# Half of a branch's activations turned by block moves and VectorE's 32x32 turns, where TensorE transposed them

## What is computed

```
h = rms_norm(x);  z = h @ w_in
u = gelu(z_u);  v = layer_norm(gelu(z_v))
A = u * (W_s v + b)             # per chunk of 128 positions and group of 128 channels
B = multi-head latent attention, 16 heads
x = x + w_out( sigmoid(g_A) * (A @ P_A) + sigmoid(g_B) * (B @ P_B) )
x = x + channel mixer           # dense SwiGLU in layer 0, top 2 of 8 experts in layer 1
```

## Time and profile before

| | |
|---|---|
| median of 3 runs | 1416.42 us |
| the profiled execution | 1416.22 us |
| its span | 1414.5 us |
| TensorE busy | 1406.1 us (99%) |
| VectorE busy | 1166.8 us (82%) |
| ScalarE busy | 951.0 us (67%) |
| GpSimd busy | 170.2 us (12%) |
| DMA | 424.32 MB, mean 300 GB/s |

### The profile page before, as it was taken

How to read it: one execution, slowest core, us unless ns; L and a number is a source line. 1 busy time by engine, 2 the same in 40 slices (tenths; PEclk the granted TensorE clock), 3 DMA queues, 4 the chain that set the end, 5 groups by cost and what they waited for, 6 DMA issues and landing times.

```text
span 1414.5 us, 19105 instructions
## 1 busy us (share of the span) xinstructions
PE 1406.1 (99%) x6575; PEld 1161.6 (82%) x6575; DVE 1166.8 (82%) x1196; ACT 951.0 (67%) x968; POOL 170.2 (12%) x302
## 2 busy tenths in 40 slices
PE   9999999999999999999999999999999999999998
PEld 7888778888888888788888888888888888888886
DVE  6998766676647899667989898898998988989986
ACT  6678645445445677644777787777877777777775
POOL 2032003476500050000300000000000000000010
PEclk9999999999999999999999999999999999999999
DMA  9476548976665484558899999999999999999995
GB/s 335 162 220 207 177 151 329 298 233 201 201 221 187 161 243 130 207 165 327 312 360 410 365 392 409 373 387 407 352 410 384 377 406 372 390 374 394 409 356 204
DMA packets 171587, 424.32 MB, mean 300 GB/s; under 512 B 19388, under 2 KB 50744, under 8 KB 171496
## 3 DMA queue, kind: packets, MB, share of 16 engines
q1 hardware_dynamic: 157128, 393.42, 76.5%
q0 software_dynamic: 13328, 26.16, 6.2%
q10 hardware_dynamic: 1040, 3.68, 0.6%
HBM read 398.20 MB, written 15.81 MB: 293 GB/s over the span
## 4 chain that ended last, share of the span: by engine, by line
PE 95%; DMA 2%; DVE 1%; ACT 1%; issue 1%; POOL 1%; SPq 0%; ACTq 0%; DVEq 0%; POOLq 0%
PE ps L620 87%; DMA raw_more<-in_moe_w_down 1%; PE ps L1187 1%; PE ps L1046 1%; PE ps L1055 1%; PE ps L925 1%; PE ps L1044 1%; PE ps L1030 1%; PE ps L969 1%; ACT w_hi L550 1%; DVE w_lo L555 1%; POOL hid_blocks L881 0%; PE ps L1003 0%; DMA hid_blocks<-hid 0%; PE ps L942 0%
## 5 line engine op out<-in xcount | busy, mean ns | idle before, releaser
L555 DVE TENSOR_TENSOR w_lo<-raw,w_hi 128x2048 fp32r<-128x2048 f32 (+3 forms) x184 | 383.7, 2093 | 81.9 <-ACT w_hi L550 80.6
L550 ACT ACTIVATE w_hi<-raw 128x2048 fp32r<-128x2048 f32 (+3 forms) x184 | 322.3, 1758 | 126.0 <-PE ps L620 102.1
L620 PE MATMUL ps<-w_hi,act_hi 128*128 128x512 f32 (+1 forms) x1264 | 332.4, 391 | 0.1
L620 PE MATMUL ps<-w_hi,act_lo 128*128 128x512 f32 (+1 forms) x1264 | 328.4, 387 | 0.0
L620 PE MATMUL ps<-w_lo,act_hi 128*128 128x512 f32 (+1 forms) x1264 | 326.6, 387 | 0.0
L620 PEld LDWEIGHTS ps<-w_lo,act_hi 128*128 128x128 f32 x1264 | 235.8, 188 | 48.1
L620 PEld LDWEIGHTS ps<-w_hi,act_lo 128*128 128x128 f32 x1264 | 235.6, 188 | 47.9
L620 PEld LDWEIGHTS ps<-w_hi,act_hi 128*128 128x128 f32 x1264 | 233.1, 188 | 46.1 <-ACT act_hi L1330 0.5
L555 DVE TENSOR_TENSOR w_lo<-raw_more,w_hi 128x2048 fp32r<-128x2048 f32 (+1 forms) x96 | 201.8, 2110 | 30.0 <-ACT w_hi L550 30.0
L550 ACT ACTIVATE w_hi<-raw_more 128x2048 fp32r<-128x2048 f32 (+1 forms) x96 | 170.1, 1775 | 54.4 <-PE ps L620 50.7
L555 DVE TENSOR_TENSOR w_lo<-raw_low,w_hi 128x2048 fp32r<-128x2048 f32 (+1 forms) x64 | 137.6, 2156 | 13.7 <-ACT w_hi L550 13.1
(11 more groups left out here) (294 smaller groups left out, 1356.1 us busy)
## 6 DMA issues: line engine op xcount, KB each, us to landing
raw<-in_moe_w_gu SPq DMA_DIRECT2D x96, 512.0 KB, 11.7
raw_more<-in_moe_w_down SPq DMA_DIRECT2D x80, 512.0 KB, 10.2
raw<-in_w_in SPq DMA_DIRECT2D x66, 512.0 KB, 5.3
raw_low<-in_moe_w_gu SPq DMA_DIRECT2D x64, 512.0 KB, 12.0
raw_more<-in_moe_w_gu SPq DMA_DIRECT2D x64, 512.0 KB, 12.5
raw<-in_moe_w_gu SPq DMA_DIRECT2D x48, 384.0 KB, 9.6
raw<-in_dense_w_gu SPq DMA_DIRECT2D x34, 512.0 KB, 5.2
raw_lent<-in_moe_w_gu SPq DMA_DIRECT2D x32, 512.0 KB, 11.4
```

Of the source, the lines that this page charges most:

```text
L550: nc.scalar.activation(w_hi[:, self.split_slot(j), 0:n], self.raw(j)[:, 0:n], ACT.Copy).then_inc(self.hi, 1)
L555: nc.vector.tensor_tensor(w_lo[:, c, 0:n], self.raw(j)[:, 0:n], w_hi[:, c, 0:n].bitcast(F32), ALU.subtract).then_inc(self.lo, 1)
L620: return nc.tensor.matmul(dst, a, b, start=start and n == 0, stop=stop and n == 2)
```

## The change

Half 0 of the branch, in both layers, is no longer transposed by TensorE; half 1 still is. ScalarE writes the biased values of half 0 into `vbuf` in another order of columns (each run of 128 channels cut into four runs of 32, so that the same run of the four groups lies together), and for that waits until both banks of `mix_tokens` are done. VectorE's product of half 0 is made in eight pieces. GpSimd's queue then copies 16 blocks of 32 partitions to `u_buf`, whose first half is free by then, with 32 KB each in runs of 512 bytes. In a new step `a_blocks`, after the argument product of "u" 1 and before the softmax product of pair 1, VectorE transposes the 32 x 32 blocks of these 128 x 1024 elements into a part of `kb`. In a new step `a_split`, at the end of the steps behind the first chunk of "gb" 1, ScalarE copies them to `t1_hi` and VectorE writes the difference to `t1_lo`, in two instructions each. The product "pa" 0 waits for these, not for the turns. Some semaphores of the router are merged into two that count up; their order of events is the same. Left out below are those renamings.

```diff
@@ -213,11 +213,11 @@
         mul(l, "u", 0, 4, [("u_arg", l, 0), split("split_hi"), ("blocks", l, "k", 0), ("u_gelu", l, 0), ("branch", l, 0)],
             split=False)
         mul(l, "u", 1, 0, [*slot(1, exps=False), ("split_lo", l, len(chunks) - 2), split("split_hi")], split=False)
-        mul(l, "u", 1, 4, [("u_square", l, 1), *slot(2, exps=False), ("u_arg", l, 1), ("softmax", l, 1)], split=False,
-            inside=[(2, ("a_turns", l, 0)), (2, ("softmax", l, 0)), (2, ("last_q", l, "q", 1)),
+        mul(l, "u", 1, 4, [("u_square", l, 1), *slot(2, exps=False), ("u_arg", l, 1), ("a_blocks", l, 0), ("softmax", l, 1)], split=False,
+            inside=[(2, ("softmax", l, 0)), (2, ("last_q", l, "q", 1)),
                     (5, ("split_lo", l, len(chunks) - 2)), (5, split())])
         mul(l, "gb", 1, 0, [("values", l, 0), split("split_hi"), *slot(3, values=False, exps=False), ("u_gelu", l, 1),
-                            ("branch", l, 1), ("blocks", l, "k", 1)], split=False, inside=[(4, ("u_tanh", l, 1))])
+                            ("branch", l, 1), ("blocks", l, "k", 1), ("a_split", l, 0)], split=False, inside=[(4, ("u_tanh", l, 1))])
         mul(l, "gb", 1, 4, [("values", l, 1), ("split_lo", l, len(chunks) - 2), *slot(4, values=False, exps=False), split("split_lo"), ("softmax", l, 3), evac("gb", 1)], split=False,
             inside=[(2, ("exps", l, 2)), (5, ("a_turns", l, 1)), (7, ("norm_probs", l, 2)),
                     (7, split("split_hi"))])
@@ -380,6 +380,9 @@
+        branch_moved = u_buf[:].rearrange("p j t n -> p j (t n)").rearrange("p j (t b k i) -> p j t b k i", t=TT, b=4, k=4)
+        branch_turned = kb[:].rearrange("p t g h d -> p (t g h d)")[:, 4 * STRIP:6 * STRIP]
+        branch_by_tile = branch_turned.rearrange("p (t b k i) -> p t b k i", t=TT, b=4, k=4)
@@ -468,6 +471,8 @@
+        a_moved, a_turned, a_hi, a_lo = (
+            [sem(f"a_moved{j}") for j in range(1)], sem("a_turned"), sem("a_hi"), sem("a_lo"))
@@ -625,6 +630,12 @@
+        BY_BLOCKS = 1
+        def branch_by_block(j):
+            return vbuf[:, :, j * STRIP:(j + 1) * STRIP].rearrange("p t (c k i) -> p t c k i", c=4, k=4)
@@ -671,7 +682,7 @@
-                    "pa": lambda: last_turn["a_turns", l, half],
+                    "pa": lambda: None if half < BY_BLOCKS else last_turn["a_turns", l, half],
@@ -858,12 +869,18 @@
+                for j in range(BY_BLOCKS):
+                    pool.wait_ge(branch_a, 2 * l + j + 1)
+                    for b in range(4):
+                        for c in range(4):
+                            pool.dma_start(branch_moved[32 * c:32 * c + 32, j, :, b, :, :],
+                                           branch_by_block(j)[32 * b:32 * b + 32, :, c, :, :]).then_inc(a_moved[j], 16)
-                    nc.gpsimd.memset(zeros, 0.0).then_inc(zeroed, 1)
-                    pool.wait_ge(zeroed, 1)
+                    nc.gpsimd.memset(zeros, 0.0).then_inc(ident_ready, 1)
+                    pool.wait_ge(ident_ready, 4)
@@ -1061,7 +1078,10 @@
+                    blocked = what == "pa" and not j and k0 // 4 < BY_BLOCKS
+                        if blocked:
+                            pe.wait_ge(a_hi, BY_BLOCKS * l + k0 // 4 + 1)
@@ -1089,6 +1109,8 @@
+                        elif p == 1 and not cell and blocked:
+                            pe.wait_ge(a_lo, BY_BLOCKS * l + k0 // 4 + 1)
...
@@ -1439,11 +1461,23 @@
-                            op = nc.scalar.activation(vbuf[:, :, gg * P:(gg + 1) * P],
-                                                      ps[:, 4 + bb % 2, g * S:(g + 1) * S].rearrange(
-                                                          "p (t d) -> p t d", t=TT),
-                                                      ACT.Identity, bias=b_sp[:, l, gg:gg + 1], scale=0.5)
+                            if step[2] < BY_BLOCKS:
+                                if not b and not g:
+                                    act.wait_ge(turn_done, bb + 2)
+                                dst, src = branch_by_block(step[2])[:, :, :, 2 * b + g, :], "p (t c i) -> p t c i"
+                                src = ps[:, 4 + bb % 2, g * S:(g + 1) * S].rearrange(src, t=TT, c=4)
+                            else:
+                                dst = vbuf[:, :, gg * P:(gg + 1) * P]
+                                src = ps[:, 4 + bb % 2, g * S:(g + 1) * S].rearrange("p (t d) -> p t d", t=TT)
+                            op = nc.scalar.activation(dst, src, ACT.Identity, bias=b_sp[:, l, gg:gg + 1], scale=0.5)
+                elif kind == "a_split":
+                    j = step[2]
+                    act.wait_ge(a_turned, BY_BLOCKS * l + j + 1)
+                    for t in range(TT):
+                        op = copy(t1_hi[:, 4 * j:4 * j + 4, t * P:(t + 1) * P].rearrange("p k (b i) -> p k b i", b=4),
+                                  branch_by_tile[:, t].rearrange("p b k i -> p k b i"))
+                    op.then_inc(a_hi, 1)
@@ -1926,9 +1960,30 @@
-                        op = stt(vbuf[:, t, cols], u_buf[:, j, t, :], mix_scale[:, ONE, t:t + 1], vbuf[:, t, cols],
-                                 ALU.mult, ALU.mult)
+                        if j < BY_BLOCKS:
+                            for k in range(4):
+                                v = branch_by_block(j)[:, t, :, k, :]
+                                op = stt(v, u_buf[:, j, t, k * P:(k + 1) * P].rearrange("p (c i) -> p c i", c=4),
+                                         mix_scale[:, ONE, t:t + 1], v, ALU.mult, ALU.mult)
+                        else:
+                            op = stt(vbuf[:, t, cols], u_buf[:, j, t, :], mix_scale[:, ONE, t:t + 1], vbuf[:, t, cols],
+                                     ALU.mult, ALU.mult)
+                elif kind == "a_blocks":
+                    j = step[2]
+                    dve.wait_ge(a_moved[j], 16 * 16 * (l + 1))
+                    if not j:
+                        dve.wait_ge(k_moved[1], 16 * 4 * DG * (l + 1))
+                    nc.vector.transpose(branch_turned, u_buf[:, j].rearrange("p t n -> p (t n)")).then_inc(a_turned, 1)
+                elif kind == "a_split":
+                    j = step[2]
+                    dve.wait_ge(a_hi, BY_BLOCKS * l + j + 1)
+                    for t in range(TT):
+                        k, cols = slice(4 * j, 4 * j + 4), slice(t * P, (t + 1) * P)
+                        op = tt(t1_lo[:, k, cols].rearrange("p k (b i) -> p k b i", b=4),
+                                branch_by_tile[:, t].rearrange("p b k i -> p k b i"),
+                                t1_hi[:, k, cols].bitcast(F32).rearrange("p k (b i) -> p k b i", b=4), ALU.subtract)
+                    op.then_inc(a_lo, 1)
```

More of the change, by code:

```diff
@@ L478, in decoder_trunk @@
         merged_b, sig_done = sem("merged_b"), sem("sig_done")
-        counting_ready, router_ready = sem("counting_ready"), sem("router_ready")
-        zeroed, rows_zeroed, gain_landed, pick_ready, rows_ready, rows_written = (
-            sem("zeroed"), sem("rows_zeroed"), sem("gain_landed"), sem("pick_ready"), sem("rows_ready"),
+        router_ready, routed_by_pe, routed_by_act = sem("router_ready"), sem("routed_by_pe"), sem("routed_by_act")
+        LOGITS_DONE, LOGITS_TURNED, PLACES_DONE = 1, 2, 3
+        COUNTING_READY, LOGITS_COPIED, GAP_EXP = 1, 2, 3
+        rows_zeroed, gain_landed, pick_ready, rows_ready, rows_written = (
+            sem("rows_zeroed"), sem("gain_landed"), sem("pick_ready"), sem("rows_ready"),
             sem("rows_written"))
@@ L486, in decoder_trunk @@
         hid_turned, hid_copied, hid_split = sem("hid_turned"), sem("hid_copied"), sem("hid_split")
-        logits_copied, logits_turned = sem("logits_copied"), sem("logits_turned")
-        logits_done, chosen_ready, gap_ready, gap_exp, places_done, places_read, counts_ready = (
-            sem("logits_done"), sem("chosen_ready"), sem("gap_ready"), sem("gap_exp"), sem("places_done"), sem("places_read"),
-            sem("counts_ready"))
+        chosen_ready, gap_ready, places_read, counts_ready = (
+            sem("chosen_ready"), sem("gap_ready"), sem("places_read"), sem("counts_ready"))
         pass_sems = []
@@ L1152, in _ @@
                                           stop=half == 1)
-            mm.then_inc(logits_done, 1)
+            mm.then_inc(routed_by_pe, 1)
             keep_busy(5)
-            pe.wait_ge(logits_copied, 1)
+            pe.wait_ge(routed_by_act, LOGITS_COPIED)
             for t in range(TT):
                 mm = nc.tensor.matmul(ps[:, 5, t * E:(t + 1) * E], logit_t[:, t * P:(t + 1) * P], stack[:], start=True, stop=True)
-            mm.then_inc(logits_turned, 1)
+            mm.then_inc(routed_by_pe, 1)
             keep_busy(14)
-            pe.wait_ge(counting_ready, 1)
+            pe.wait_ge(routed_by_act, COUNTING_READY)
             pe.wait_ge(chosen_ready, 1)
@@ L1167, in _ @@
             nc.tensor.matmul(ps[:, 3, 2 * E:3 * E], ones_r, chosen[:, 0, :], start=True, stop=False)
```

(16 more changed lines are left out.)

## The result

The kernel after takes 1421.77 us (median of 6 runs, 1420.35 to 1423.12), the kernel before beside it 1416.36 (6 runs, 1415.75 to 1416.96). The ratio is 1.0040, 95% interval 1.0029 to 1.0051: slower by 5.4 us. The forecast was 1418.8, half of that loss, with 0.58 for a change within 0.2% and 0.38 for slower, which it was.

The account below looks back on a forecast made before the run. TensorE bounds the kernel, but VectorE has no slack where they meet, so the saved 0.94 us a layer is lost; 1.25 us a layer, 2.5 for both, on 1416.22 or 1416.42 gave 1418.8 us, range 1414.8 to 1422.6.

Parts of the forecast that it names:

- The bound: Third pass of the "u" 1 chunk: TensorE and VectorE's w_lo arrive together, margin 0.09 us; a shorter TensorE queue moves nothing.
- The rival in which TensorE keeps what it saves: Transposes' 1.88 us for both layers kept: 1414.4 us; a part kept: 1415.6; chance 0.15 for part or all.
- The pieces: VectorE's branch product: eight pieces take 2.15 us instead of 1.42, +0.7, so the third pass starts at 125.75.
- The a_split in front of t_lo: VectorE, second half: 1.2 us of added queue delays the value product of pair 1 to 145.75, +1.25 us a layer.
- the 0.25 us stall: TensorE's wait for VectorE's softmax of pair 1, forecast to vanish while y is under 0.65.
- punctual moves: Moves landing early enough that y is under 0.65, so TensorE does not wait for the softmax of pair 1.
- Again no margin: Value product of pair 1 at 144.52: first t_lo ends about 144.15, just when TensorE is there, marked 0.35 wait.
- The landing: GpSimd's 16 moves: last issue at 130.45, 4.25 us to landing, landed at 134.7, bounds 133.4 and 136.9.
- y: VectorE's wait for the moves in front of the new transpose: 0.5 us, range 0 to 2.7.
- the rival of late moves: Landing 6.4 us after the last issue, y = 2.7, a layer costs 3.4 us: 1423.2 us; chance 0.30.
- the sum for y over 0.5: Delay of the value product of pair 1, a layer's cost: 0.75 + y instead of 1.25 us.
- The moves share the DMA engines with the loads of gm_w_proj: ScalarE takes the first loaded chunk only at 136.93 without waiting for data; sharing costed at nothing.

Follow-up runs that it names:

- the turns alone: Kernel before with only TensorE's eight transposes of half 0 gone, so its product uses unturned numbers: 1415.38 us, ratio 0.9997.
- no moves: Kernel after without the 16 moves and VectorE's wait for them, so half 0 never reaches "pa" 0: 1419.2 us, ratio 1.0022 to the kernel before.
- the order mended: Kernel after with moves on two queues (GpSimd, SyncE) and the k transpose of half 1 behind the scores of pair 3: 1417.15 us, ratio 1.0006.
- the last version: Kernel after with two queues, later k transpose, and ScalarE applying the position scale so the branch product is two 128x512 instructions: 1415.38 us, ratio 0.9997.
- the loads are held: Kernel after with SyncE waiting for all 16 moves before issuing the next loads of gm_w_proj: 1420.02 us, one run.

## Why the forecast had the mechanism right and the cost too small

**The bound, right.** TensorE and VectorE arrive together at the third pass, and a shorter TensorE queue moves nothing: the turns alone are worth 0.25 us a layer, not 0.94. The rival in which TensorE keeps what it saves was out for this reason. The Trainium skill ("VectorE: DVE Perf Modes", section "Rules for kernel authors") advises TensorE for a 128x128 turn whose result may lie in PSUM. The prediction took from this that the removal is worth nothing, which the page does not say; the run gives it 0.25 of 0.94 us.

**The pieces, right.** 2.15 us forecast, 2.19 measured; the third pass at 125.75 forecast and 125.75 measured. Taking the pieces back shortened the stretch by 0.9 and 0.57 us.

**The a_split in front of t_lo, right.** With the moves out of the way (no moves), the value product of pair 1 starts 25.43 us into the stretch; the forecast, 145.75, is 25.26. A layer then costs 1.42 us where 1.25 were forecast, and the 0.25 us stall is gone, as forecast for punctual moves. One reading was off: "Again no margin". The 0.35 at 144.52 was no wait, and where TensorE does wait for t_lo its product starts 0.16 us behind it (145.67 to 145.83, no moves), so the margin was about 0.2 us, not nothing. The two costs named are enough: with the order mended 27.24 are left in layer 0, with the pieces mended as well 26.35.

**The landing, the term that was mis-sized.** This is "I take 4.25: landed at 134.7". The last issue came at 130.7 (forecast 130.45), but to landing it took 6.0 us and y, VectorE's wait, was 2.54 and 2.25, not 0.5. This is the rival of late moves, which had a chance of 0.30, y = 2.7 and 1423.2; it came true nearly in full. The measured 1421.77 lies inside the range because the range took in most of this rival, not because the central sum was right. The two layers lost 3.00 and 2.72 us; the sum for y over 0.5, 0.75 + y, gives 3.29 and 3.00, so the mechanism stood and was 0.3 us too dear.

The prediction read two rows by size (16 KB at 3.0, 64 KB at 6.0, the medians) and took a value between them for 32 KB. The median of all 16 did come out at 4.3, but by luck: it lies between six moves at 1.8 and ten at 4.8. And a median was the wrong number to take, since VectorE waits for the last landing; the most in the earlier trace rows, 4.8 and 6.4, would have put it between those two, by my estimate at about 5.6. What size hid was the traffic. The sentence "The moves share the DMA engines with the loads of gm_w_proj" saw the loads, but asked only whether they would be late, not what they would do to the moves. The rows that it read for a price had been taken beside loads as well, as the windows of the kernel before show for the 64 KB moves of the earlier trace rows and the first 32 of 16 KB:

```profile
107.20:113.60 6.40, 6.40 (x30) 5.31 (x29) 5.51 (x3) 4.32 (x4) 6.36 (x12) 1.00 1.06 289
263.80:280.00 16.20, 16.20 (x73) 13.44 (x72) 10.04 (x12) 7.75 (x9) 15.68 (x32) 1.00 0.92 286
```

The Trainium skill ("DMA: Bandwidth & Descriptors", section "Anatomy of one DMA — SWDGE (gpsimd) path") gives 2.0 us plus bytes over 436e9 a second, an estimate of 2.1 us for 32 KB. The moves of layer 0 when the loads are held, 1.7 to 2.2, agree with it, and so do the six ahead of the loads in the kernel after, 1.7 to 2.4. Beside the loads the measurement, 4.0 to 6.0, decides against it. The prediction was right to leave it out of the sum, but saw in it a question of size and not of traffic.

**What the sum of the parts says.** From after to before, layer 0: 29.80, less 1.58 for the moves' lateness, less 0.98 for the order around the a_split, less 0.89 for the pieces, is 26.35, the stretch of the last version, where the kernel before has 26.80. These are steps from one run to the next, so they add up by themselves; that the costs are separate is shown by the order, which is worth 0.99 us beside late moves and 0.95 to 1.00 without them. What the change wins when all three are mended is 0.45 us in layer 0 and 0.09 in layer 1, and with the wait for bt_lo behind the stretch (0.40 in place of 0.26) about 0.3 and nothing, less than can be measured in 1416. The chip's answer is that half of the turns were not worth taking off TensorE here, since VectorE sets the pace of this stretch.

## What to carry to other kernels

Where two engines arrive at a point together, price a removal on one of them at nothing until the other's queue has room. When a transfer becomes something that an engine waits for, cost its last landing and not the median, and look at what else the DMA engines carry between its issue and its due time, as well as at its size; issue it earlier, or let the load that can wait go second. Work that loses its cover must be placed by its next two deadlines: behind the first it may only be late for the second.

## What the runs showed of the hardware that I had not expected

- Small moves suffer from large loads by more than a factor of two. A move of 32 KB from SBUF to SBUF took 1.7/1.8/2.2 us (least, median, most of the 16 in layer 0) with the loads held and the DMA engines at 0.26 busy. In the kernel after the six issued ahead of the loads took 1.7/1.8/2.4, and the ten behind the first load 4.0/4.8/6.0, at 0.81 and above.
- TensorE's granted clock fell to its lower level, 0.50, twice in the traces of this case, apart from the end of the program: for some 3.3 us each, behind its two longest idle times, in which its weight loads waited 2.04 and 2.33 us. At half speed that is some 1.7 us of TensorE's time lost, on top of the wait. Behind the wait of 1.95 us in the kernel after it stayed at 1.00.
- A 128x512 product with a four-dimensional order of columns (L1980) took 1.29 us for two, and one with a scalar factor in plain order 1.42: no cost shows for an inner run of 32 elements, though the two differ in the operation as well. Cutting each of the two instructions in four cost VectorE 0.77 us (2.19 against 1.42), and TensorE 0.53 to 0.9.
- GpSimd spends 0.54 us on the issue of such a move; SyncE spent 2.67 us on four, and 5.2 to 6.3 on eight, so SyncE's queue is no faster for small ones.
